# Scores of two attention branches from two products instead of three

## What is computed

```python
for layer in range(DEPTH):
    u = rms_norm(h, norm_pre[layer])
    (a_cq, a_ckv, a_kr, a_g, b_q, b_k, b_v, b_g, c_q, c_k, c_v, c_qi, c_ki, c_wi, c_g,
     d_q, d_k, d_v, d_g) = jnp.split(u @ w_in[layer], split_at, axis=-1)
    y_a = mla_branch(...) * silu(a_g)              # latent attention
    y_b = dilated_branch(b_q, b_k, b_v, bias_b) * silu(b_g)
    y_c = sparse_branch(c_q, c_k, c_v, c_qi, c_ki, c_wi, bias_c, k_top) * silu(c_g)
    y_d = diff_branch(...) * silu(d_g)             # two softmax maps
    h = h + rms_norm(jnp.concatenate([y_a, y_b, y_c, y_d], -1) @ w_out[layer], norm_post[layer])
```

## Time and profile before

| | |
|---|---|
| median of 3 runs | 691.1 us (691.07 to 691.25) |
| span of the profiled execution, first to last instruction | 689.9 us |
| the profiled execution's own time | not given apart from its span |
| PE busy | 665.3 us, 96% |
| VectorE busy | 394.1 us, 57% |
| ScalarE busy | 338.7 us, 49% |
| GpSimd busy | 241.9 us, 35% |
| mean granted clock of TensorE | 0.999 of full |
| HBM read and written | 69.77 MB and 13.94 MB |

### The profile page before, as it was taken

One profiled execution on the slowest core, in us unless ns is written; L12 is line 12 of the kernel. 1 busy time (PEld: TensorE's weight loads), 2 busy tenths in 40 slices (PEclk: granted clock), 3 DMA queues, 4 the chain that ended last, 5 costly groups with the idle time before them and its releaser, 6 DMA issues. The chain is left out here.

```text
span 689.9 us, 10538 instructions
## 1 busy us (share of the span) xinstructions
PE 665.3 (96%) x3852; PEld 538.4 (78%) x3852; DVE 394.1 (57%) x982; ACT 338.7 (49%) x804; POOL 241.9 (35%) x209
## 2 busy tenths in 40 slices
PE   6999999999999999999999999999999999999996
PEld 4988877788887665679998897878788777556995
DVE  4413599868669375540470257985968755555114
ACT  5523634666333647952353355456543553787120
POOL 1442541434242942002424534325422467020030
PEclk9999999999999999999999999999999999999999
DMA  8448877323222213012362697552322220120202
GB/s 252 138 169 223 240 216 254 124 78 109 76 77 77 78 61 123 1 43 82 124 183 76 214 273 207 146 152 77 110 77 76 77 78 23 58 104 1 92 31 92
DMA packets 68763, 80.97 MB, mean 117 GB/s; under 512 B 12853, under 2 KB 54453, under 8 KB 68713
## 3 DMA queue, kind: packets, MB, share of 16 engines
q1 hardware_dynamic: 68713, 80.31, 38.1%
HBM read 69.77 MB, written 13.94 MB: 121 GB/s over the span
## 5 line engine op out<-in xcount | busy, mean ns | idle before, releaser
L684 POOL TENSOR_TENSOR w_low<-w_raw,w_high 128x512 fp32r<-128x512 f32 (+2 forms) x156 | 199.8, 1313 | 364.2 <-ACT w_high L726 364.1
L1236 PE MATMUL bank<-uT,w_high 128*128 128x512 f32 x400 | 159.7, 399 | 0.0
L1238 PE MATMUL bank<-uT,w_low 128*128 128x512 f32 x400 | 157.8, 394 | 0.0
L1237 PE MATMUL bank<-uT,w_high 128*128 128x512 f32 x400 | 157.4, 393 | 0.0
L834 ACT ACTIVATE probs<-probs,negmax 128x128 f32<-128x128 f32 (+3 forms) x160 | 88.8, 557 | 51.6 <-DVE negmax L1085 50.4
L726 ACT ACTIVATE w_high<-w_raw 128x1024 fp32r<-128x1024 f32 (+2 forms) x78 | 76.4, 1031 | 28.5 <-DMA w_raw<-in_w_out 24.4
L1236 PEld LDWEIGHTS bank<-uT,w_high 128*128 128x128 f32 x400 | 75.2, 188 | 17.4 <-issue 1.4
L1238 PEld LDWEIGHTS bank<-uT,w_low 128*128 128x128 f32 x400 | 75.0, 188 | 17.7
L1237 PEld LDWEIGHTS bank<-uT,w_high 128*128 128x128 f32 x400 | 75.2, 188 | 16.2
L1236 PE MATMUL bank<-w_high,mix 128*128 128x256 f32 x256 | 72.1, 282 | 0.2 <-DVE gate L1095 0.2
L1237 PE MATMUL bank<-w_low,mix 128*128 128x256 f32 x256 | 71.6, 280 | 0.0
(11 more groups left out here) (153 smaller groups left out, 1048.1 us busy)
## 6 DMA issues: line engine op xcount, KB each, us to landing
w_raw<-in_w_in SPq DMA_DIRECT2D x27, 1024.0 KB, 5.5
w_raw<-in_w_out SPq DMA_DIRECT2D x8, 1024.0 KB, 4.9
parts_dram<-staging SPq DMA_DIRECT2D x12, 512.0 KB, 5.6
strips<-strips_dram SPq DMA_DIRECT2D x24, 256.0 KB, 5.6
dqk<-parts_dram SPq DMA_DIRECT2D x24, 256.0 KB, 4.4
hX<-in_x SPq DMA_DIRECT2D x8, 512.0 KB, 5.4
qidx<-parts_dram SPq DMA_DIRECT2D x12, 256.0 KB, 4.3
w_raw<-in_w_in SPq DMA_DIRECT2D x4, 512.0 KB, 5.6
```

The costliest lines, as they stand in the source:

```text
L684: ins = nc.gpsimd.tensor_tensor(w_low[:, s, ks, 0:w], w_raw[:, s, ks, 0:w], w_high[:, s, ks, 0:w].bitcast(F32), ALU.subtract)
L1236: nc.tensor.matmul(out_ap, lh, rh, start=start, stop=False)
L1237: nc.tensor.matmul(out_ap, lh, rl, start=False, stop=False)
L1238: return nc.tensor.matmul(out_ap, ll, rh, start=False, stop=stop)
```

## The change

The queries and keys of B and C are kept in another form. For each head there is now a tile of 128 partitions: the query tile `bqq` (or `cqq`) holds the head's high query part twice, in both halves of the partitions; the key tile `bkk` (`ckk`) holds the high key part in the head's own half and the low key part in the other. One product over 128 partitions is then high x high plus high x low. The low query parts have tiles of their own (`bqlow`, `cqlow`), and the second product, over 64 partitions, is low x high. To write these, ScalarE makes four copies of 64 partitions for a query unit and two for a key unit, in place of one of 128; VectorE makes two differences of 64 partitions in place of one. Four tiles of 2 KB a partition take the low queries: two lie in the second half of `staging`, one in `kidx`, one in a new room. Waits are as they were.

```diff
@@ tiles @@
+        room("low", 2 * KB)
-        cqk = at("cqk", "X", [P, 2, 2, 2, SEQ], F32R)
-        bqk = at("bqk", "Y", [P, 2, 2, 2, SEQ], F32R)
+        cqq, ckk = (at(n, "X", [P, HEADS, SEQ], F32R, skip=8 * KB * i) for i, n in enumerate(("cqq", "ckk")))
+        bqq, bkk = (at(n, "Y", [P, HEADS, SEQ], F32R, skip=8 * KB * i) for i, n in enumerate(("bqq", "bkk")))
+        bqlow = [at(f"bqlow{c}", "staging", [P, SEQ], F32R, skip=4 * KB + 2 * KB * c) for c in range(2)]
+        cqlow = [at(f"cqlow{c}", ("kidx", "low")[c], [P, SEQ], F32R) for c in range(2)]
@@ ScalarE, kind == "unit" @@
                         if step[1:] in STACKED:
                             dst = staging[:, STACKED.index(step[1:]) % 2, 0, :]
+                            nc.scalar.activation(dst, b, ACT.Copy, scale=scale).then_inc(high_written, 1)
+                        elif name in ("ck", "bk"):
+                            for half in range(2):
+                                rows = slice(HD * half, HD * (half + 1))
+                                ins = nc.scalar.activation((ckk if name == "ck" else bkk)[rows, 2 * c + half, :], b[rows, :],
+                                                           ACT.Copy)
+                            ins.then_inc(high_written, 1)
                         else:
-                            qk = cqk if name[0] == "c" else bqk
-                            dst = qk[:, int(name[1] == "k"), 0, c, :]
-                        nc.scalar.activation(dst, b, ACT.Copy, scale=scale).then_inc(high_written, 1)
+                            for half in range(2):
+                                for to in (half, 1 - half):
+                                    ins = nc.scalar.activation(
+                                        (cqq if name == "cqq" else bqq)[HD * to:HD * (to + 1), 2 * c + half, :],
+                                        b[HD * half:HD * (half + 1), :], ACT.Copy, scale=scale)
+                            ins.then_inc(high_written, 1)
@@ VectorE, kind == "unit" @@
-                            qk = cqk if name[0] == "c" else bqk
-                            hi, lo = (qk[:, int(name[1] == "k"), part, c, :] for part in range(2))
-                        ins = nc.vector.scalar_tensor_tensor(lo, b, scale, hi.bitcast(F32), ALU.mult, ALU.subtract)
+                            for half in range(2):
+                                rows = slice(HD * half, HD * (half + 1))
+                                if name in ("ck", "bk"):
+                                    both = (ckk if name == "ck" else bkk)[:, 2 * c + half, :]
+                                    hi, lo = both[rows, :], both[HD * (1 - half):HD * (2 - half), :]
+                                else:
+                                    hi = (cqq if name == "cqq" else bqq)[rows, 2 * c + half, :]
+                                    lo = (cqlow if name == "cqq" else bqlow)[c][rows, :]
+                                ins = nc.vector.scalar_tensor_tensor(lo, b[rows, :], scale, hi.bitcast(F32),
+                                                                     ALU.mult, ALU.subtract)
@@ TensorE, kind == "scores" @@
-                            qk = cqk if br == "C" else bqk
+                            qq, kk, low = (cqq, ckk, cqlow) if br == "C" else (bqq, bkk, bqlow)
                             rows = slice(HD * (h % 2), HD * (h % 2) + HD)
-                            ins = three(b, qk[rows, 0, 0, h // 2, qs], qk[rows, 0, 1, h // 2, qs],
-                                        qk[rows, 1, 0, h // 2, ks], qk[rows, 1, 1, h // 2, ks], True, True)
+                            nc.tensor.matmul(b, qq[:, h, qs], kk[:, h, ks], start=True, stop=False)
+                            ins = nc.tensor.matmul(b, low[h // 2][rows, qs], kk[rows, h, ks], start=False, stop=True)
```

More of the change, by code:

```diff
@@ L1039, in _ @@
                             s = STACKED.index(step[1:])
-                            hi, lo = staging[:, s % 2, 0, :], staging[:, s % 2, 1, :]
-                        else:
-                            qk = cqk if name[0] == "c" else bqk
-                            hi, lo = (qk[:, int(name[1] == "k"), part, c, :] for part in range(2))
-                        ins = nc.vector.scalar_tensor_tensor(lo, b, scale, hi.bitcast(F32), ALU.mult, ALU.subtract)
+                            ins = nc.vector.scalar_tensor_tensor(staging[:, s % 2, 1, :], b, scale,
+                                                                 staging[:, s % 2, 0, :].bitcast(F32),
+                                                                 ALU.mult, ALU.subtract)
+                        else:
+                            for half in range(2):
[7 more added lines that the diff above has]
+                                ins = nc.vector.scalar_tensor_tensor(lo, b[rows, :], scale, hi.bitcast(F32),
+                                                                     ALU.mult, ALU.subtract)
                     ins.then_inc(emptied_by["dve"], 1)
```

## The result

The changed kernel takes **704.3 us** (median of 4 runs, 700.5 to 707.5) against 691.1 us in the runs of the kernel before that stood beside it: a ratio of 1.020 (1.016 to 1.024), slower by 13 us where 2 us of gain were forecast. One run of the kernel of experiment 1 (2217.6 us) and one of the kernel before beside it (2748.6 us) lie far outside and are left out of every range.

What follows compares the result with a forecast made beforehand. The prediction took PE's instruction stream to bound the kernel: 5.05 us saved a layer, less 3.9 of waits and 0.15 unseen, made 1.0 a layer, 2.0 in all, so 689.1 us, range 685.5 to 694.2.

Steps and rivals of the forecast that it cites:

- rows of the array cost nothing: B's and C's score products on PE: widening the first from 64 to 128 rows adds no cost, leaving 10.1 us saved.
- if it lost half of what it saves: Fallback for the widened first product on PE: should it cost half the saving, 5 us would stay.
- 3.9 us a layer: Sum of PE's waits at the projection units behind the smaller copies and differences, set against 5.05 us saved a layer.
- bq 1: +1.2: Behind query unit bq 1, ScalarE's late copies of turned probabilities hold a bank, so bk 0 starts 1.2 us later.
- bk 0: +1.1: Behind key unit bk 0, VectorE's shift that frees a score bank comes later, costing PE 1.1 us.
- bk 1: +0.8: Behind key unit bk 1, late VectorE shifts cost 0.8 us: three score blocks save nothing, cqq 0 starts 0.4 later.
- cqq 0: +0.6: Behind query unit cqq 0, late copies and differences free the bank cqq 1 needs later, costing PE 0.6 us.
- ck 0, ck 1 and bv 0: After cqq 1, little lateness: ck 0 adds 0.2 us through late turned copies, ck 1 is covered by bv 0.
- (a): Rival: stalls at bq 1, bk 0 and cqq 0 are absorbed, the whole 10.1 us comes out, 681.0 us; chance 0.09.
- (c): Rival: PE waits for every unit, all 13 us of lateness a layer, + 16 net, 707 us; chance 0.03.
- (d): Rival: weight loads run in series with streams, each removed product gives 0.11 us more, 682.1 us; chance 0.03.
- (b): Rival: in C's stretch PE waits for turned copies, losing C's 2.5 us a layer, +2.8, 693.9 us; chance 0.13.

Runs made afterwards that it cites:

- experiment 1: Changed kernel with its second product over all 128 partitions instead of 64: 692.3 us, ratio 1.001 to the kernel before.
- experiment 3: Kernel before without the second of its three products, copies as before: 682.2 us, ratio 0.987.
- experiment 5: Changed kernel with 6 and 7 idle products added on PE at two places of each layer where it waits for VectorE: 702.2 us, ratio 1.015.
- experiment 6: Changed kernel with the edits of experiment 1 and experiment 5 together: 685.7 us, ratio 0.991 to the kernel before.
- experiment 7: Changed kernel, ScalarE's copies all reading and writing at partition 0, both products on the same 64 rows, scores mixed up: 690.5 us, ratio 0.999.

## Why the prediction was wrong

- **The price of a removed product was right, its condition wrong.** The step that failed is "rows of the array cost nothing" in what PE loses. It took a product of 128 rows from a run of 128-row products and one of 64 from a run of 64-row products, and never the two in turn. 10.1 us were to be gained; alternation took all of it and 0.75 us a layer more behind bv 0. Equal row counts give 8.9 us (experiment 3) or 12 us behind bv 0 (experiment 1). The Trainium skill has this rule (TensorEngine Tiling (Array Packing), "Key Properties": "Mode switching requires drain"); the traces agree, with 0.31 to 0.42 us a product in place of 0.12 to 0.23. The rule of the Trainium skill that the prediction did weigh, on loads and row groups, was rightly refused: the loads of 64-row products of one head do begin before their own product (203.46 for the one at 203.58). The fallback "if it lost half of what it saves" was a size with no row behind it.
- **The term for the clock was missing.** Every duration was taken at the full clock, as the earlier trace rows had it. That was the clock of a PE which, after its first 15 us, never waited longer than 0.8 us. From bk 0 on, 5.4 us in layer 0 and 1.2 in layer 1 are units at half clock, and 0.6 more lies inside bk 0's step. The changed kernel's runs spread roughly with it: 700.5 us at a mean clock of 0.996, 702.8 at 0.990, 705.7 at 0.991, 707.5 at 0.985.
- **The waits were named rightly and sized too low.** The sum was 3.9 us a layer, which counts what the products are no longer able to save; net of that the prediction had cqq 1 "some 3.2" late. This is what the starts measure: 4.4 and 4.8 without the units' lengths, and 4.4 in layer 0 of experiment 5 at the full clock. The step "bq 1: +1.2" became 1.62: copies at 0.60, not 0.50, and the bank that VectorE frees came last, not the turned copy. "bk 0: +1.1" measured 1.4. "bk 1: +0.8" was to make cqq 0 start 0.4 later and measured 0.93. "cqq 0: +0.6" measured -0.17 in the changed kernel and 0.47 in experiment 5; the wait itself is there once the products are quick, 1.2 us in experiments 1 and 6. The 0.50 and 0.60 were pitches of operations that start on one partition. That ck 0, ck 1 and bv 0 add nothing of note came true (-0.12 in all).
- **The rivals.** (a), (c) and (d) did not occur. (b) had the sign and not the reason: PE's waits for turned copies stayed at 3.6 us in 10. The time lies above the range, since two of its three causes, alternation and clock, were in no case.

The sum against the profiled span: start-up -1.4 (layer 0 -1.05, layer 1 -0.33), waits 9.2 (0.6 of it half clock before bk 0 of layer 0), units at half clock 6.6, the scores behind bv 0 +1.5, between cqq 1 and bv 0 -0.2; together the 15.8 measured. The 10.1 that did not come stand in no row of it, and that was the largest error. Part of the 15.8 is chance: 707.5 is the longest of four runs, and the shortest, 700.5, would have left 7 us less to explain.

## What to carry to other kernels

Before a product is widened to save another, look at the row counts of what stands next to it in the instruction stream: here equal ones overlapped and alternating ones did not. Price a cut into partial partitions by a row with the same changes of first partition, or leave the engines whole tiles and let DMAs move the halves where there is time before their use. Where a change adds waits to a PE that had none, look at the granted clock behind each, and price the matmuls behind it at both levels.

## What the runs showed that was not expected

- A product of 64 rows and one of 128 in turn cost 0.31, 0.37 and 0.42 us at 256, 384 and 512 columns, where equal ones cost 0.12, 0.17 and 0.23, whether both have 64 or both 128.
- ScalarE's copies of 64 partitions and 512 columns stand 0.60 us apart with a changing first partition and 0.48 with one and the same. VectorE's differences of 64 partitions stand 0.70 apart with a changing first partition and 0.61 with one and the same (the key units of experiment 7), which is the pitch of whole tiles. For VectorE the Trainium skill has this rule (VectorE: DVE Perf Modes, "Two Vector instructions with no wait between them"): an instruction that starts in another group of 32 partitions than the one before it begins only when all before it have finished. The traces agree with it on VectorE.
- The granted clock fell to its lower level behind waits of PE of 1.4 and 1.9 us, and with those waits filled by idle products it did not fall there in the traced executions. It also fell 2 us behind waits of 0.5 us and less (168.9), and did not fall behind one of 1.9 us in layer 1 of the changed kernel (497.4) or behind the 1.25 us before cqq 1 in experiment 6. Why it fell at some waits and not at others stays open.
